# Two gates and two branch projections computed by tokens over 512 output columns, with their gated sum turned afterwards

## The reference, cut to what matters

```
proj = hn @ w_in                      # gate_fox and gate_gdn are two of its 1024-column parts
y = sigmoid(gate_fox) * (y_fox @ w_branch_fox) + sigmoid(gate_gdn) * (y_gdn @ w_branch_gdn)
h = h + y @ w_out
```

## Time and profile before

| What | Value |
|---|---|
| Median of 3 runs | 806.86 us (806.81 to 808.23) |
| Profiled execution | 807.0 us, its span from the first to the last instruction 805.6 us |
| TensorE busy | 798.9 us, 99% of the span |
| VectorE busy | 592.9 us, 74% |
| ScalarE busy | 448.9 us, 56% |
| GpSimd busy | 74.4 us, 9% |

### The profile page before, as it was taken

How to read it: one execution, slowest core, us unless ns; L and a number is a source line. 1 busy time by engine, 2 the same in 40 slices (tenths; PEclk the granted TensorE clock), 3 DMA queues, 4 the chain that set the end, 5 groups by cost and what they waited for, 6 DMA issues and landing times.

```text
span 805.6 us, 13987 instructions
## 1 busy us (share of the span) xinstructions
PE 798.9 (99%) x5608; PEld 721.3 (90%) x5608; DVE 592.9 (74%) x1001; ACT 448.9 (56%) x729; POOL 74.4 (9%) x65
## 2 busy tenths in 40 slices
PE   8999999999999999999999999999999999999998
PEld 6999998999999989899999998887878888888887
DVE  6888878875454776769999996486766777778543
ACT  6666577554535554556656564366665655655441
POOL 0001000010011203001101110021100111011000
PEclk9999999999999999999999999999999999999999
DMA  7855564547432554575687655555425656656542
GB/s 261 241 163 162 178 228 145 172 121 223 126 114 86 175 170 158 200 241 179 196 253 242 221 191 203 171 194 166 148 81 169 204 176 207 190 177 208 184 162 73
DMA packets 126257, 144.15 MB, mean 179 GB/s; under 512 B 11488, under 2 KB 103024, under 8 KB 125936
## 3 DMA queue, kind: packets, MB, share of 16 engines
q1 hardware_dynamic: 123744, 141.22, 55.1%
q10 hardware_dynamic: 2448, 2.03, 1.0%
HBM read 141.78 MB, written 1.46 MB: 178 GB/s over the span
## 4 chain that ended last, share of the span: by engine, by line
PE 97%; DMA 1%; DVE 1%; ACT 1%; SPq 0%; issue 0%; DVEq 0%; ACTq 0%
PE bank L579 94%; DMA panel_raw<-in_w_in 1%; PE bank L633 1%; PE bank L943 0%; DVE panel_lo L1557 0%; PE bank L665 0%; PE bank L892 0%; ACT panel_hi L1080 0%; PE bank L916 0%; PE bank L720 0%; ACT x_halves L1080 0%; PE bank L822 0%; SPq L2358 0%; DVE h L1986 0%; DVE h L1998 0%
## 5 line engine op out<-in xcount | busy, mean ns | idle before, releaser
L1557 DVE TENSOR_TENSOR panel_lo<-panel_raw,panel_hi 128x1024 fp32r<-128x1024 f32 x251 | 313.5, 1252 | 144.8 <-ACT panel_hi L1080 144.2
L579 PE MATMUL bank<-x_halves,panel_hi 128*128 128x256 f32 (+1 forms) x1952 | 416.0, 305 | 1.0 <-DVE x_halves L1993 0.7
L1080 ACT ACTIVATE panel_hi<-panel_raw 128x1024 fp32r<-128x1024 f32 (+1 forms) x253 | 266.8, 1057 | 164.2 <-PE bank L579 160.7
L579 PEld LDWEIGHTS bank<-x_halves,panel_hi 128*128 128x128 f32 x1952 | 315.8, 191 | 16.9 <-issue 0.9
L579 PE MATMUL bank<-x_halves,panel_lo 128*128 128x256 f32 x1152 | 324.8, 282 | 0.0
L579 PEld LDWEIGHTS bank<-x_halves,panel_lo 128*128 128x128 f32 x1152 | 219.8, 191 | 0.0
L579 PE MATMUL bank<-panel_hi,x_halves 128*128 128x512 f32 x256 | 80.6, 396 | 0.0
L579 PE MATMUL bank<-panel_hi,act_hi 128*128 128x512 f32 x176 | 68.6, 390 | 0.0
L579 PE MATMUL bank<-panel_hi,act_lo 128*128 128x512 f32 x176 | 68.5, 389 | 0.0
L579 PE MATMUL bank<-panel_lo,act_hi 128*128 128x512 f32 x176 | 68.5, 389 | 0.0
L579 PEld LDWEIGHTS bank<-panel_hi,x_halves 128*128 128x128 f32 x256 | 46.8, 188 | 9.9 <-DVE panel_lo L1557 0.6
(11 more groups left out here) (289 smaller groups left out, 927.6 us busy)
## 6 DMA issues: line engine op xcount, KB each, us to landing
panel_raw<-in_w_in SPq DMA_DIRECT2D x38, 1024.0 KB, 5.3
panel_raw<-in_w_up SPq DMA_DIRECT2D x30, 1024.0 KB, 5.4
panel_raw<-in_w_down SPq DMA_DIRECT2D x20, 1024.0 KB, 5.1
panel_raw<-in_w_gate SPq DMA_DIRECT2D x10, 1024.0 KB, 5.3
panel_raw<-in_w_out SPq DMA_DIRECT2D x8, 1024.0 KB, 5.0
panel_raw<-in_w_in SPq DMA_DIRECT2D x11, 512.0 KB, 4.6
panel_raw<-in_w_branch_fox SPq DMA_DIRECT2D x4, 1024.0 KB, 4.9
panel_raw<-in_w_branch_gdn SPq DMA_DIRECT2D x4, 1024.0 KB, 5.2
```

The source lines that it names most:

```text
L579: return e.matmul(o, l, r, start=start, stop=stop, skip_group_check=True)
L1080: return e.activation(o, i_, ACT.Copy, scale=scale)
L1557: e.tensor_tensor(lo, raw_view(i, k0, kt), hi.bitcast(F32), ALU.subtract).then_inc(s_lo, 1)
```

## The change

The gates and the branch projections are made in the `wide` form: two products each of four steps instead of four of two. `BOTH_HALVES` with its additions goes. `gate_f` and `gate_g` lie with tokens on the partitions, and so does their sum, so TensorE turns it (`turn_y`): eight transposes of 128 x 128 after step 86 and eight after step 90, into side banks. ScalarE and VectorE take the high and low part from there. `out` is reordered, so that it takes the first half of the sum for both column halves in steps 89 to 92, and the second half in steps 93 to 96. ScalarE's tanh stands directly behind the `split` of the step, ahead of that step's other work. The two banks of a gate product are handed out in reversed order.

```
...
     for kind, x, w, c0 in (("gate_f", "mix", "w_in", C_GF), ("gate_g", "mix", "w_in", C_GG),
                            ("branch_f", "yf", "w_branch_fox", 0), ("branch_g", "yg", "w_branch_gdn", 0)):
-        for j in range(4):
-            out.append(((kind, j), x, "hl" if (kind, j) in BOTH_HALVES else "fm", w, 0, KD, c0 + j * PW, PW))
-    for c in range(2):
-        for k in (0, HALF):
+        for c in range(2):
+            for k in (0, HALF):
+                add_wide((kind, c), x, w, k, HALF, c0 + c * WIDE)
+    for k in (0, HALF):
+        for c in range(2):
             add_wide(("out", c), "y", "w_out", k, HALF, c * WIDE)
...
                 if first:
-                    for target in targets:
+
+                    for target in targets[::-1] if key[0] in ("gate_f", "gate_g") else targets:
                         bank_for(ring_of(key), target)
...
+            def turn_y(j):
+                key = ("y_turn", j)
+                b3 = pairs(side(key))
+                for s, v in room(key):
+                    e.wait_ge(s, v)
+                e.wait_ge(s_mixed, TT * (j // 2 + 1))
+                for k in range(2):
+                    for m in range(TT):
+                        f = 2 * j + k
+                        i_ = e.transpose(b3[:, k, m * P:(m + 1) * P], gate_g[:, m, f * P:(f + 1) * P], ident)
                 i_.then_inc(will_fill(key), 1)
...
+                for c in range(2):
+                    if n == END["branch_g", c] + 2:
+                        for j in (2 * c, 2 * c + 1):
+                            turn_y(j)
...
-            def gate(kind, j, dst):
-                e.wait_ge(*product((kind, j)))
-                e.activation(dst[:, 2 * j:2 * j + 2, :], pairs(bank_of((kind, j))), ACT.Tanh,
-                             scale=0.5).then_inc(empties((kind, j)), 1)
...
+            def gate(kind, c, dst):
+                for m in range(TT):
+                    e.wait_ge(*product_of((kind, c), m))
+                    e.activation(dst[:, m, wide(c)], bank_of((kind, c, m)), ACT.Tanh, scale=0.5) \
+                        .then_inc(empties((kind, c, m)), 1)
 
             def mix_hi(j):
-                e.wait_ge(s_mixed, j + 1)
-                copy(yh[:, 2 * j:2 * j + 2, :], gate_g[:, 2 * j:2 * j + 2, :]).then_inc(s_y_hi, 1)
+                e.wait_ge(*filled(("y_turn", j)))
+                copy(yh[:, 2 * j:2 * j + 2, :], pairs(bank_of(("y_turn", j)))).then_inc(s_y_hi, 1)
...
                 split(n + 3)
+                for c in range(2):
+                    if n == END["gate_f", c]:
+                        e.wait_ge(s_rows_out, 16)
+                        e.wait_ge(s_gc_rows_out, 16)
+                        e.wait_ge(s_blk_back[0], 16)
+                        e.wait_ge(s_blk_back[1], 16)
+                        gate("gate_f", c, gate_f)
+                    if n == END["gate_g", c]:
+                        gate("gate_g", c, gate_g)
...
-                e.tensor_tensor(d, sums, d, ALU.mult).then_inc(s_branch, 1)
+            def branch(kind, c, gates, s_gate):
+                for m in range(TT):
+                    d = gates[:, m, wide(c)]
+                    e.wait_ge(s_gate, TT * c + m + 1)
+                    e.wait_ge(*product_of((kind, c), m))
+                    e.tensor_tensor(d, bank_of((kind, c, m)), d, ALU.mult).then_inc(empties((kind, c, m)), 1)
...
```

More of the change, by code:

```diff
@@ L246, in build @@
         gz = at("gz", [P, TT, D], 24)
-        gate_f = at("gate_f", [P, KD, T], 0)
-        gate_g = at("gate_g", [P, KD, T], 11)
+        gate_f = at("gate_f", [P, TT, D], 0)
+        gate_g = at("gate_g", [P, TT, D], 11)
         yg_halves = at("yg_halves", [P, 2, HEADS, T], 17, F32R)
         ygh, ygl = yg_halves[:, 0], yg_halves[:, 1]
-        low = [at(f"branch_low{i}", [P, 2, T], 10, skip=2048 * i) for i in range(3)]
         h = at("h", [P, TT, D], 24)
@@ L550, in build @@
                 "pooled": (mixh, mixl)}
-        HALVES_OF = {"norm2": x_halves, "yf": yf_halves, "yg": yg_halves}
+        HALVES_OF = {"norm2": x_halves}
         def x_ready(x, kx):
@@ L1476, in scalar_program @@
                             fox_project(kind, j)
[L1477 to L1490, removed]
+                for c in range(2):
+                    if n == END["branch_g", c] + 2:
+                        for j in (2 * c, 2 * c + 1):
+                            mix_hi(j)
                 for x, kind, gain, first in (("ffn", "out", "norm_ffn", 2), ("norm1", "down", "norm1", 4),
@@ L1808, in fox_lo @@
                                 ALU.subtract).then_inc(empties(("fox_y", hh)), 1)
[L1810 to L1824, removed]
-                e.tensor_tensor(d, sums, d, ALU.mult).then_inc(s_branch, 1)
+            def branch(kind, c, gates, s_gate):
[4 more added lines that the diff above has]
+                    e.tensor_tensor(d, bank_of((kind, c, m)), d, ALU.mult).then_inc(empties((kind, c, m)), 1)
             def mix_lo(j):
                 e.wait_ge(s_y_hi, j + 1)
-                e.tensor_tensor(yl[:, 2 * j:2 * j + 2, :], gate_g[:, 2 * j:2 * j + 2, :],
-                                yh[:, 2 * j:2 * j + 2, :].bitcast(F32), ALU.subtract).then_inc(s_y, 1)
+                e.tensor_tensor(yl[:, 2 * j:2 * j + 2, :], pairs(bank_of(("y_turn", j))),
+                                yh[:, 2 * j:2 * j + 2, :].bitcast(F32), ALU.subtract).then_inc(empties(("y_turn", j)), 1)
             def add_to_h(kind, c):
@@ L2164, in vector_program @@
                             e.tensor_copy(vf[:, m, wide(j)], bank_of(("fv", j, m))).then_inc(empties(("fv", j, m)), 1)
[L2165 to L2172, removed]
+                for c in range(2):
+                    if n == END["branch_f", c]:
+                        branch("branch_f", c, gate_f, s_gate_f)
+                    if n == END["branch_g", c]:
+                        branch("branch_g", c, gate_g, s_gate_g)
+                    if n == END["branch_g", c] + 2:
+                        for j in (2 * c, 2 * c + 1):
+                            mix_lo(j)
                 for x, kind, gain, first in (("ffn", "out", "norm_ffn", 2), ("norm1", "down", "norm1", 4),
@@ L2266, in mask_key_bias, with affine @@
                 i_.then_inc(s_kb, 1)
[L2268 to L2271, removed]
+            def affine(kind, c, dst, s_done):
+                for m in range(TT):
+                    d = dst[:, m, wide(c)]
+                    e.wait_ge(*emptied((kind, c, m)))
+                    e.tensor_scalar(d, d, 0.5, 0.5, ALU.mult, ALU.add).then_inc(s_done, 1)
             def gained():
@@ L2309, in pool_program @@
                     mask_key_bias(FOX_AT[n - 1] + 1)
[L2310 to L2319, removed]
+                for c in range(2):
+                    if n == END["gate_f", c]:
+                        affine("gate_f", c, gate_f, s_gate_f)
+                    if n == END["gate_g", c]:
+                        affine("gate_g", c, gate_g, s_gate_g)
+                    if n == END["branch_g", c]:
+                        for m in range(TT):
+                            d_f, d_g = gate_f[:, m, wide(c)], gate_g[:, m, wide(c)]
+                            e.wait_ge(*emptied(("branch_f", c, m)))
+                            e.wait_ge(*emptied(("branch_g", c, m)))
+                            e.tensor_tensor(d_g, d_g, d_f, ALU.add).then_inc(s_mixed, 1)
                 if n == END["out", 1] + 1:
```

23 lines of the change are left out of this document (5 added, 18 removed).

## The result

The changed kernel takes 809.91 us (median of 8 runs, 808.38 to 811.43) against 806.90 us for the kernel before: a ratio of 1.0028 with a 95% interval of 1.0016 to 1.0039. It is slower by 3.0 us, 0.3%, and outside the range I gave. The profiled execution took 808.38 us with a span of 806.9 us.

The account below looks back on a forecast made before the run. TensorE, busy 99% of the span, was taken as the bound. Saved 3.2 + 0.6 + 0.3 = 4.1 us, added 1.8 + 2.1 + 0.95 = 4.85 us, net +0.75 us: median 807.6 us, range 806.5 to 808.9 us.

Parts of the forecast that it names:

- the clock at the wait of step 57: Rival: TensorE's clock falls to 1.2 GHz after the 2.1 us wait, one step costing 2.7 us more, 810.3 us; 6%.
- the loss behind small products: Steps 57 to 72: late first large matmuls lose equally in both forms, counted as nothing; 0.9 us kept as dear-side bound.
- What bounds the kernel: TensorE, busy 99% of the span, sets the time; its added work or waits count in full.
- What the wide form saves: Gate and branch steps 57 to 88: 3.2 us from `fm` steps and 0.6 us from `hl` steps, together 3.8 us.
- The stall in `out`: A late matmul of `out`, caused by ScalarE waiting for GpSimd's sum, counted as gone: 0.3 us saved.
- The turning: Two added groups of eight transposes on TensorE, 0.80 us each and 0.08 us behind each: 1.8 us in all.
- Step 57: First rows of `gate_f` wait for ScalarE to empty the keys' bank 1 with the copy to `kfT`: 2.1 us.
- step 73: `branch_f` waits for the last gate's tanh to empty bank 0: 0.85 us and 0.1 us slow start, 0.95 us.
- The sum's path: From step 84, GpSimd's sums done at about 7.5 us, transposes at 8.16 us: no cost, 0.6 us to spare.
- the late sum: Rival: GpSimd's sums come late and both transpose groups wait 0.5 us each, 808.6 us; 16% together with slow starts.
- The sum: Whole kernel: 4.1 us saved, 4.85 us added, net +0.75 us; 807.75 us profiled, 807.6 us median.
- The free bank as a rival: Rival: first gate finds its bank free, step 57 waits 0.6 us and step 73 not at all, 805.2 us; 8%.

Follow-up runs that it names:

- the late tanh: Changed kernel with plain bank order and keys copied first, plus the gates' tanh back at the end of ScalarE's work for the step: 812.10 us, ratio 1.0059.
- both repairs: Changed kernel with plain order of the gates' banks and ScalarE's copy of the keys at the start of its step 56 work: 805.41 us, ratio 0.9982.
- the plain order of banks: Changed kernel with the first rows of each gate in bank 0 and the second in bank 1, not reversed: 806.24 us, ratio 0.9984.
- the kernel before with the waits: Kernel before the change, with only the first gate's bank moved to bank 1 and so on in turn, without the wide form: 810.99 us, ratio 1.0038.
- reversed for `gate_f` only: Changed kernel with reversed banks for `gate_f` but not `gate_g`, keeping the wait at step 57 and removing that at 73: 809.26 us, ratio 1.0019.
- the repaired kernels: Changed kernel with keys copied at the start of ScalarE's step 56 work: banks still reversed, 806.52 us; with plain banks, 805.41 us.

## Why the prediction was wrong

**The step that failed is the clock at the wait of step 57.** The forecast left it at 1.00 behind 2.1 us of rest and gave the fall 6%. It fell in 10 of 14 executions of the changed kernel, which costs about 1.4 us. A second term was mis-sized: the loss behind small products was put at nothing and measured 0.7 us. Together they are 2.1 of the 2.3 us between the forecast of 807.6 and the median of 809.91 us. The executions at full clock took 808.4 to 808.9 us, inside the range. The waits and the turning came out as worked out.

- **What bounds the kernel**: right. With each experiment's waits counted at full length, the executions at full clock came within 0.4 us of what was expected in every experiment but the late tanh, which has none.
- **What the wide form saves**: the distances between starts were right (0.120 and 0.227 us). **The mis-sized term is the slow start, "I take the loss as equal".** A gate step between small products lost 0.14 us against its pure twelve matmuls, in `fm` 0.08 us, so the step gave 0.10 us and not 0.16 us. In that step the first distance is longer by 0.08 to 0.09 us in both forms; in `wide` nine more lie between 0.224 and 0.236 us, mostly 0.23 or more, before they settle at 0.227. Over the sixteen steps 1.85 us are saved instead of 2.56 us, 0.7 us short. I had the rows and put 0.9 us into the bound on the dear side instead of into the sum.
- **The stall in `out`**: right. Five steps of `out` in the changed kernel take 13.70 us from 328.58 on, 5 x 2.72 and 0.10 for the start: nothing is late there.
- **The turning**: 0.79 us and the start behind it, as worked out, twice.
- **Step 57**: 2.1 us forecast, 2.15 us measured; **step 73**: 0.95 us forecast, 0.89 us and 0.08 us of slow start measured. The steps in between wait for nothing.
- **The sum's path**: right with more to spare, 1.3 us instead of 0.6; the late sum did not happen. Two sums in a row took 3.54 us, less than twice 2.14 us as counted.
- **The sum**: +0.75 us forecast, +1.4 us in the profiled execution (808.38 against 807.0). The 0.7 us of slow starts are the difference.
- **The clock** is what put the median outside the range. I had it as a rival with 6%, because a rest of 1.5 us in the trace had left the clock at 1.00, and took that row as evidence for 2.1 us. The row is one execution of a shorter rest: at the same place of the start-up the profiled execution with both repairs rested 1.64 and then 0.66 us, and there the clock fell. The price was over-sized: 2.7 us for one step, against 1.4 us measured for a stretch of 3.4 us. The median is then that of the executions with a fall: 808.4 to 808.9 us and about 1.4 us. That the profiled execution lies inside the range is luck: it is one of the four in fourteen without a fall.
- **The free bank as a rival**: its mechanism is what the plain order of banks does, at 806.24 us; I had 805.2 us, too low by the same 0.7 us of slow starts and 0.3 us more.

The page on TensorE in the Trainium skill ("TensorE: Matmul & The Clock Gate", What's actually happening) has the clock at half after an idle stretch. The trace of the kernel before with the waits agrees, 0.50 behind a rest of 2.1 us; that of the changed kernel shows 1.00 behind the same rest. By the formula that the Trainium skill has under Back-to-back issue gap on that page, there called the gap of a single matmul, the wide form would hardly pay. The version with both repairs, 1.7 us faster after 1.8 us of transposes and 0.7 us of slow starts, decides for the rows. For a stream of matmuls with weight loads that section of the Trainium skill gives about 131 ns at 512 columns; the rows here show 227 ns.

## What to carry to other kernels

When a product is cut into fewer and longer groups, work out from the order which bank each group's first matmul takes and who empties it: with two banks in turn, the first rows should go to the bank that has been free longest, and here one reversed list cost 3.7 us. A wait on a TensorE that is otherwise always busy cost its length where it was 1.3 us, and in most executions the clock as well where it was 2.1 us. Then the time spreads from execution to execution, and one profile may show none of it, so look at the granted clock of every run. Count a wider matmul's gain from steps in the surroundings where it will stand, not from its steady pace.

## What the runs showed of the hardware

- With a rest of about 2.1 us in the stream of matmuls 28 of 37 executions had a mean clock under 1.000. The trace that caught it behind step 57's wait shows 1.2 GHz for 3.4 us. Three profiled executions with the same wait (the changed kernel twice, reversed for `gate_f` only once) stayed at full clock. With a rest of 1.3 us 3 of 11 were low, near the rate of the kernel before, which has no such rest.
- The kernel before was low in 14 of 67 executions, at 807.7 to 810.3 us. No trace caught one of them. In the two low executions of the repaired kernels that were profiled the clock fell in the first 30 us, behind rests of 1.92 us (for a panel's low part) and of 1.64 and 0.66 us (for the first activations); that the falls of the kernel before lie there too is likely and not shown. Not all its slow executions are low: others at full clock took up to 808.7 us.
- At 1.2 GHz a matmul with its weight load takes 0.213 us instead of 0.120 us with 256 columns, and 0.43 us instead of 0.23 us with 512: less than twice as long.
- Behind small products, matmuls of 512 columns with new weights each need up to ten starts to come back to their pace. Those of 256 columns need one, apart from a few hundredths of a microsecond. The first distance is longer by 0.08 us behind the attention's turns and values and by 0.19 us behind its scores (`kfT`, `qfT`), in both forms.
